# A diffusion layer on eight cores: a Fourier row fetched earlier, weights and tokens asked for one by one, and a gating moved behind a weight fetch

## Time and profile before

| what | us |
|---|---|
| median of three runs | 1690.61 (1689.73 to 1691.33) |
| the profiled execution's own time | 1697.91 |
| its span, from the first to the last instruction, on its slowest core (core 2) | 1696.4 |
| spans of the eight cores | 1680.1 to 1696.4 |
| PE busy | 1551.4 (91%) |
| DVE busy | 841.5 (50%) |
| ACT busy | 578.6 (34%) |
| POOL busy | 414.9 (24%) |

### The profile page before, as it was taken

The page is one execution under the profiler, slowest core; times in us unless marked ns, Lnnn a source line. Parts: engine busy times, 40 slices in busy tenths (PEclk is TensorE's granted clock), DMA queues, the critical chain, the costliest instruction groups (busy, mean ns, idle before and its releaser), DMA issues.

```text
span 1696.4 us, 27654 instructions; the slowest of 8 cores (1680.1 to 1696.4 us)
## 1 busy us (share of the span) xinstructions
PE 1551.4 (91%) x8936; PEld 782.8 (46%) x9084; DVE 841.5 (50%) x1229; ACT 578.6 (34%) x1000; POOL 414.9 (24%) x236
## 2 busy tenths in 40 slices
PE   0279989997899899989999999999999999999997
PEld 0145434444677676434444444444444444444443
DVE  0067687775688576466233333333333333333346
ACT  1055254334789797005311111111111111111145
POOL 1000045432001000040404412442144314441320
PEclk9999999999999999999999999999999999999999
DMA  9999997757375964955335254434534353525524
GB/s 172 186 270 240 166 135 116 118 76 111 67 133 119 169 117 76 230 70 82 54 52 97 51 100 72 77 63 88 93 58 81 69 100 51 99 50 100 89 76 159
DMA packets 90401, 183.73 MB, mean 108 GB/s; under 512 B 3858, under 2 KB 62994, under 8 KB 86802
## 3 DMA queue, kind: packets, MB, share of 16 engines
q0 software_dynamic: 78640, 142.65, 52.7%
q1 hardware_dynamic: 11620, 39.31, 6.9%
HBM read 316.20 MB, written 8.39 MB: 191 GB/s over the span
## 4 chain that ended last, share of the span: by engine, by line
PE 76%; DMA 15%; DVE 5%; issue 2%; ACT 2%; POOL 0%; DVEq 0%; ACTq 0%; POOLq 0%; SPq 0%
PE psum L284 75%; DMA arena<-w_ada 9%; DMA arena<-x_own 2%; DVE arena L291 2%; DMA arena<-dft_alt 1%; DMA arena<-w_in 1%; DMA arena<-w_out 1%; PE psum L288 1%; DVE arena L432 1%; DVE arena L644 1%; ACT arena L392 0%; ACT arena L1056 0%; ACT arena L429 0%; DVE arena L816 0%; DVE arena L1053 0%
## 5 line engine op out<-in xcount | busy, mean ns | idle before, releaser
L284 PE MATMUL psum<-arena 128*128 128x512 bf16 (+3 forms) x8256 | 1520.6, 346 | 118.2 <-DMA arena<-w_ada 78.1
L284 PEld LDWEIGHTS psum<-arena 128*128 128x128 bf16 (+1 forms) x8404 | 742.6, 99 | 866.1 <-issue 161.7
L291 DVE TENSOR_TENSOR arena<-psum,arena 128x512 f32<-128x512 f32 (+2 forms) x594 | 403.2, 715 | 617.0 <-PE psum L284 574.5
L291 POOL TENSOR_TENSOR arena<-arena 128x2048 bf16<-128x2048 bf16 (+1 forms) x102 | 308.2, 3035 | 329.4 <-DMA arena<-w 221.5
L1135 ACT ACTIVATE arena<-psum 128x512 f32<-128x512 f32 x128 | 75.3, 588 | 661.9 <-PE psum L284 661.9
L890 ACT ACTIVATE arena<-psum 128x768 bf16<-128x768 f32 x288 | 223.6, 810 | 49.0 <-PE psum L284 42.3
L281 POOL DMA_DIRECT2D arena<-w_ada x48 | 34.4, 718 | 401.1 <-PE psum L284 161.0
L291 DVE TENSOR_TENSOR arena<-arena 128x256 f32<-128x256 f32 (+3 forms) x159 | 113.8, 717 | 33.1 <-DMA arena<-w 14.5
L816 DVE SCALAR_TENSOR_TENSOR arena<-arena 128x1024 f32<-128x1024 bf16 x94 | 117.3, 1275 | 8.9 <-DMA arena<-w_ada 8.4
L392 ACT ACTIVATE arena<-arena 128x2048 bf16<-128x2048 f32 x26 | 49.7, 1910 | 205.7 <-DVE arena L291 103.0
L281 POOL DMA_DIRECT2D arena<-w x24 | 25.4, 1058 | 267.9 <-PE psum L284 191.9
(11 more groups left out here) (52 smaller groups left out, 279.4 us busy)
## 6 DMA issues: line engine op xcount, KB each, us to landing
arena<-w_ada POOLq DMA_DIRECT2D x48, 1024.0 KB, 15.6
arena<-w POOLq DMA_DIRECT2D x24, 2048.0 KB, 15.5
arena<-x_own SPq DMA_DIRECT2D x16, 1024.0 KB, 19.0
arena<-w_in POOLq DMA_DIRECT2D x7, 2048.0 KB, 20.7
arena<-w POOLq DMA_DIRECT2D x8, 1536.0 KB, 11.6
arena<-x_oth SPq DMA_DIRECT2D x8, 1024.0 KB, 12.4
out<-arena SPq DMA_DIRECT2D x16, 512.0 KB, 3.4
arena<-w_out POOLq DMA_DIRECT2D x3, 2048.0 KB, 29.4
```

What stands on the lines that cost most here:

```text
L284: S.add('pe', lambda e, o_=out, l=lhsT, r=rhs, a=start, b=stop, kw=kw: e.matmul(o_, lhsT=l, rhs=r, start=a, stop=b, **kw), reads=reads, wr ...
L291: S.add(eng, lambda e, o_=out, a=in0, b=in1, op=op: e.tensor_tensor(out=o_, in0=a, in1=b, op=op), reads=reads, writes=writes)
```

```diff
-            if t >= 2:
+            if t >= 4:
                 next(g4)
...
-                if cb == 0 and t == 1:
+                if cb == 0 and t == 0:
                     wslot[1] = load_wb(w_in[:, 512:1024])
...
-                if cb == 1 and t == 1:
+                if cb == 1 and t == 0:
                     wslot[2] = load_wb(w_in[:, 1024:1536])
+                if cb == 1 and t == 3:
+                    S.alias('alt', ['ropr%d' % i for i in range(4)])
+                    dma('pool', AV(P0 + 14 * KB, 2 * KB, BF16)[0:1, :], alt_d[:, :], 'alt', writes=['alt'])
...
-                if cb == 0 and t == 5:
+                if cb == 0 and t == 7:
                     make_gs(2, 4, 0, g2col, 'g2col')
                     v_rows()
                 if cb == 2 and t == 7:
+                    qk_two(len(QKU) - 1)
                     v_proj()
...
-        qk_two(NQK - 1)
...
-        ALT = AV(G(14), 2 * KB, BF16)[0:1, :]
+        ALT = AV(P0 + 14 * KB, 2 * KB, BF16)[0:1, :]
...
-        dma('pool', ALT, alt_d[:, :], 'alt', writes=['alt'])
...
-        def prefetch_wo():
+        def prefetch_wo(n):
...
                 if four_st[0] == 'end':
-                    prefetch_wo()
+                    pre = [(k + 2, 0), (k + 30, 1), (k + 55, 2), (k + 70, 3)]
+            while pre and k >= pre[0][0]:
+                prefetch_wo(pre.pop(0)[1])
...
                 if cb == 3:
+                    if t >= 5:
+                        norm2_flip(0, (range(0, 2), range(2, 5), range(5, 8))[t - 5])
                     n2[t] = norm2_stats(t)
                     if 1 <= t <= 4:
                         norm2_x(t - 1, n2[t - 1])
-                    if t >= 5:
-                        norm2_flip(0, (range(0, 2), range(2, 5), range(5, 8))[t - 5])
...
-                load_w2(0)
+                load_w2(0, 0)
             if cb == 1:
                 load_wo(3)
+                load_w2(0, 1)
```

More of the change, by code:

```diff
@@ L778, in build_program @@
         GT2 = AV(T0 + 12 * KB, 8 * KB)
-        for k in (['mixT_%d' % t for t in range(8)] + ['on0', 'on1', 'wcs', 'alt', 'onesf']
+        for k in (['mixT_%d' % t for t in range(8)] + ['on0', 'on1', 'wcs', 'onesf']
                   + ['pt%d' % i for i in range(4)] + ['abt%d_%d' % (i, j) for i in range(2) for j in range(2)]):
@@ L924, in build_program @@
         g_ada, g_four = ada_rest(), fourier()
-        def prefetch_wo():
[L926 to L931, removed]
+        def prefetch_wo(n):
+            if n < 2:
+                S.alias('wof%d' % n, ['ft'])
+                dma('pool', HFR[:, :, n * 512:(n + 1) * 512], w_out[n * 1024:(n + 1) * 1024, 0:512].rearrange("(k p) n -> p k n", p=128), 'wof%d' % n, writes=['wof%d' % n])
+            else:
+                t = n - 2
+                OLDP = ['pq%d_%d' % (v, c) for v in range(2) for c in range(4)] + ['ext', 'ada2', 'shb', 'rope3'] + ['ropr%d' % i for i in range(4)] + ['alt']
                 for kk in ACCK(t):
@@ L934, in prefetch_wo @@
                 dma('sp', ACC[t], x_own[t * 128:(t + 1) * 128, :], 'acc%d' % t, writes=ACCK(t))
+        pre = []
         flips = []
@@ L969, in build_program @@
                 if four_st[0] == 'end':
-                    prefetch_wo()
+                    pre = [(k + 2, 0), (k + 30, 1), (k + 55, 2), (k + 70, 3)]
+            while pre and k >= pre[0][0]:
+                prefetch_wo(pre.pop(0)[1])
             if pr == NPAIR - 1:
                 norm_O(ui)
-        assert four_st[0] == 'end' and not flips
+        assert four_st[0] == 'end' and not flips and not pre
         for _ in g_ada:
@@ L1003, in build_program, with load_w2 @@
         NB = 16
-        def load_w2(b):
+        def load_w2(b, part=2):
             s = b % 2
+            if part == 1:
+                return gate_w2(b)
             r0 = b * 512
@@ L1016, in load_w2, with gate_w2 @@
                 S.add('pool', fn, writes=wk, dma='w2s1', ndma=2)
+            if part == 2:
+                gate_w2(b)
+        def gate_w2(b):
+            s = b % 2
             for j in range(4):
```

## The result

| | before, us | changed, us |
|---|---|---|
| median of 13 runs each, side by side | 1691.33 | 1673.66 |
| ratio, with its 95% interval | | 0.9898 (0.9878 to 0.9918) |
| spans of the cores, profiled execution | 1680.1 to 1696.4 | 1666.6 to 1672.3 (cores 0 to 5), 1681.8 and 1685.3 (cores 6 and 7) |

The change makes the kernel 17.7 us faster (14 to 21 by the interval); 25 were forecast. In some executions of any kernel half of the cores or a pair of them take longer at a lower mean granted clock, as cores 6 and 7 do in this profile: stages of after are those of cores 0 to 5, a ratio leaves out only the longest of these executions, and a median given with a count leaves out all in which a core had less than 0.98.

A forecast was written before the change was run, and what follows sets the result against it. The chain through PE was taken as the bound, with time to gain in its waits between 200 and 830 us. Terms summed to 32.7 us on core 2 and 24.0 on core 7; 25 was taken: 1665.6 us, range 1655 to 1680.

The forecast's parts named there:

- gating behind the last `w_out`: Output stage: w_out fetched ahead of four POOL multiplications, so PE's wait goes; 5.9 us on core 2, nothing on core 7.
- a core like 7: Slowest core after the change: core 7, without core 2's w_out wait, gains 24.0 us and has 1669.6.
- rival A: Attention: bias or a w_ada block holds DVE, then PE, taking over part of the gain; 1677 us, chance 0.13.
- Fourier row: Start of attention: row asked for some 12 units ahead arrives in time; 11.8 us on core 2, 10.2 on core 7.
- one by one: Attention: w_out halves and tokens fetched singly, so the w_ada block isn't late; 8.1 us on core 2, 8.2 on core 7.
- The new wait for the gate bias: Attention: DVE newly waits for the small bias transfer on SP's queue; a loss of 0.5 us, ends 0 and 5.
- Flips: Ahead of the statistics on ACT: evacuations stand ready for PE; 4.7 us on every core, ends 2.5 and 5.5.
- an MLP as long as before: Sign, behind 830 us: the MLP's length was to stay unchanged.
- K and Q: g4 two units later, w_in one earlier, shorter waits; 3 us on core 2, 2 on core 7, ends 0 and 5.5.
- the 1 to 4 named: Sign: PE's waits for w_ada after the change were to be between 1 and 4 us.
- rival C: K: each of the five later w_ada blocks of g4 stops PE; slower, 1706 us, chance 0.03.
- the last `qk_two` ahead of `v_proj`: Before the first Fourier step: the copy delays DVE's cast; a loss of 0.3 us on core 2, 0.6 elsewhere.

The follow-up runs named there:

- The row: Kernel before with only the Fourier row asked for earlier, in the second Q column block: median 1677.52 us against 1691.05, ratio 0.9961.
- the fetch: Kernel before with only the first output weights and two token tiles asked for one by one: median 1682.03 us against 1691.05, ratio 0.997.
- the flips: Kernel before with only the flips put ahead of the statistics: median 1686.93 us against 1690.92, ratio 0.9976.
- the K and Q edits: Kernel before with only g4 two units later, w_in and v_rows moved, last qk_two ahead of v_proj: median 1692.58 us against 1690.92, ratio 1.0003.
- the one wait: Changed kernel, first w2 multiplication behind the issue waits for DVE's addition of tile 0, third column block: median 1666.18 us against 1690.92 before, ratio 0.9853.
- the gating back: Changed kernel with the four w2 multiplications ahead of the last w_out fetch again: median 1671.75 us against 1695.51 before, ratio 0.9861.
- late: Changed kernel with the four multiplications moved behind the fetch of w2's block 1, into the MLP: median 1671.02 us against 1695.51 before, ratio 0.9856.
- spaced: Changed kernel with one multiplication behind every second tile of the third column block, each awaiting DVE's addition: median 1669.83 us against 1695.51 before, ratio 0.9847.
- in pairs: Changed kernel with the four multiplications in two pairs, behind DVE's additions of tiles 1 and 5: median 1665.88 us against 1691.05 before, ratio 0.9913.
- the cut multiplication: Changed kernel with block 0's first multiplication cut into 128 and 1920 columns, no wait added: median 1667.22 us against 1690.92 before, ratio 0.9857.

## Why the prediction was right in sign and 7 us off in size

**The sum closes within 2 us.** The row, the fetch and the flips alone give -13.5 - 9.0 - 4.0 = -26.5 us, and with the +1.7 of the K and Q edits -24.8. The changed kernel with the one wait that ends the lock-out gives 1666.18 - 1690.92 = -24.7. That the four parts meet it to 0.1 is luck: the +1.7 holds a loss that the changed kernel can't have, and row and fetch shorten attention by 11.2 + 7.6 = 18.8 us alone, by 17.2 together. The changed kernel itself gives -17.7. It lacks that one wait and nothing else, so what is missing is 7.0 us in one place.

**The step that failed: gating behind the last `w_out`.** It had +5.9 on core 2, 0 on core 7. Its mechanism was right: the fetch goes out early and PE doesn't wait for it; where the gating goes back ahead of it, core 2 has 94.7 us in that stage instead of 89.2, 5.5 us. But the step followed the multiplications only to POOL's next issue and called the end of that harmless. It didn't ask what DVE does in those 16 us. Moving them made every core 8 to 9 us slower there, so the net on a core like 7 was about -8 where 0 was forecast. The row of before from which it could have been suspected was the additions of 3.8 us beside the same four multiplications; I had not read DVE there. That it would be four at once and not one by one, no row of before showed. That 1673.66 still lies in the range of 1655 to 1680 is luck in part: the range was opened for rival A, which didn't come, and not for this loss. The narrower range for a core like 7, 1659 to 1674, isn't what its ends add up to either: they give gains of 7.1 to 28.8 us, so 1662 to 1684.

**Fourier row and one by one.** Forecast 10.2 - 0.5 and 8.2 on core 7, together 17.9. Attention is shorter by 17.2 us in the mean: right. (The medians of the two parts alone give 22.5, more than forecast; where the rest came from wasn't settled.) The new wait for the gate bias was 0.31 us on core 5; 0.5 was taken:

```profile
417.96 1.28 DVE L818 SCALAR_TENSOR_TENSOR arena<-arena 128x1024 f32<-128x1024 bf16 x1 [0.31 <-DMA arena<-bgate]
```

DVE doesn't wait for `w_ada` in attention on any core, and for the bias at most 1.4 us in all (core 7) and not at all on cores 0, 2, 3 and 6, so rival A is refuted.

**Flips.** 4.7 forecast, 4.0 measured alone, within its ends. On ACT of the changed kernel, core 5, an evacuation now stands ahead of a tile's square, which answers to the earlier trace rows:

```profile
767.52 0.78 ACT L1068 ACTIVATE arena<-psum,arena 128x512 bf16<-128x512 bf16 x1 [1.09 <-PE psum L284]
768.20 1.90 ACT L392 ACTIVATE arena<-arena 128x2048 bf16<-128x2048 f32 x1
```

The stretch behind these flips, which had a granted clock of 0.50, now has 1.00 (777 to 783 us, same core). The 5.18 x 0.50 = 2.6 us that this gives back fit the 2.5 us by which the stage behind the first relu is shorter in the mean; the prediction had named an MLP as long as before as a sign.

**K and Q.** 3 and 2 us were forecast; cores 2, 3 and 5, which were late, gained 2.8 to 5.5 and cores 0, 1 and 4 at most 0.4, which fits a stage paced by DVE's chain at about 174.5 us. PE's waits for `w_ada` are 1.8 to 3.0 us on cores 1, 3, 5 and 7, within the 1 to 4 named, and none on the other four; rival C needed more than that for each block. The prediction let the first `w_ada` block's issue move "by one addition of POOL only"; that is 3.8 us, which costs nothing once the row no longer stands behind it (DVE doesn't wait for the block); without the early row PE's wait for the row grew by 3.3 us in the mean. What the part is worth beside the early row, no run shows: every version that has both the row and the fetch has it too. The price of the last `qk_two` ahead of `v_proj` was forecast at 0.6 for most cores: the L297 wait is 6.2 us with it and 4.8 to 5.6 in the runs of the row and of the fetch alone, which lack it (cores 0, 2, 4 and 7).

**Which core is slowest.** I took a core like 7 to stay slowest. After the change cores 0 to 5 lie within 5.7 us of each other, where before all eight lay within 16.3; what core 2 alone had lost is gone, as the prediction said, and with the lock-out ended the gain of the kernel, 24.7, is near the 24.0 of a core like 7.

Versions that beat both kernels: the gating back, late, spaced, in pairs, with the one wait and with the cut multiplication, by 23.7 to 25.7 us against before by the medians above (back 1695.51 - 1671.75 = 23.8, late 1695.51 - 1671.02 = 24.5, spaced 25.7, pairs 25.2, one wait 24.7, cut 1690.92 - 1667.22 = 23.7), each beside its own runs of before. Which of them is best these runs don't tell. Since the gating back is among them, this part of the change is worth some 2 us at most (25.7 - 23.8) even where it locks nothing out.

## What to carry to other kernels

When work is moved on POOL, look at what DVE does in the window it moves to: additions of two on-chip operands there can be stopped for the length of POOL's instructions, and three banks cover a hold of one instruction at a time, not of four at once. Put such POOL work where DVE reads PSUM, or break it up behind waits on DVE's own progress. And follow an edit to every transfer that stands behind it: the K and Q edits alone gained nothing, and the fetches behind the moved addition were asked for later.

## What was not expected of the hardware

An addition on DVE was held for four multiplications of POOL in a row (14.66 us, and 17.64 where it began during the issue) when they stood right behind a DMA issue of POOL; for one at a time (2.0 to 4.6 us) when there was a gap of 3 us, when the first had waited, or when a 128-column instruction stood behind the issue. While DVE was held for all four they took 16.21 us, otherwise 17.58, with DVE's additions in between. Why the instruction right behind an issue keeps DVE out beyond its own end was not settled; a version with other work than an issue ahead of the four, and nothing awaited, was not tried.
